# Key norms and low-rank inputs prepared in the value columns, and unread products in four gaps of TensorE

## What is computed

```python
h = rmsnorm(x, lp['norm1_g']) * (1.0 + sc1) + sh1
proj = h @ lp['w_in']
r_a, k_a, v_a, q_b, k_b, v_b, x_c, g_c = jnp.split(proj, SPLIT_POINTS, axis=-1)
...
kk = l2_normalize((k * lp['rwkv_kk']).reshape(shp))
for d in range(2):
    w = jnp.exp(-DECAY_SCALE * jax.nn.sigmoid(lp['rwkv_w0'][d] + jnp.tanh(h @ lp['rwkv_wA'][d]) @ lp['rwkv_wB'][d]))
    a = jax.nn.sigmoid(lp['rwkv_a0'][d] + (h @ lp['rwkv_aA'][d]) @ lp['rwkv_aB'][d])
    kd = k * (1.0 + (a - 1.0) * lp['rwkv_ka'])
    o, s_last = rwkv7_scan(rh, w, kd, vh, kk, a, s0[:, d], reverse=(d == 1))
g = jax.nn.sigmoid(h @ lp['rwkv_gA']) @ lp['rwkv_gB']
```

## Time and profile before

| | us |
|---|---|
| median of 3 runs | 4451.15 |
| the runs | 4451.15, 4453.65, 4433.3 |
| the profiled execution | 4451.32 |
| its span, first to last instruction | 4449.5 |
| mean granted clock of TensorE in it | 0.951 of full rate |
| TensorE busy | 4073.4 (92%) |
| VectorE busy | 3399.8 (76%) |
| ScalarE busy | 1590.9 (36%) |
| GpSimd busy | 1405.3 (32%) |

### The profile page before, as it was taken

The page is one execution under the profiler, slowest core; times in us unless marked ns, Lnnn a source line. Parts: engine busy times, 40 slices in busy tenths (PEclk is TensorE's granted clock), DMA queues, the critical chain, the costliest instruction groups (busy, mean ns, idle before and its releaser), DMA issues. The chain is left out here.

```text
span 4449.5 us, 71520 instructions
## 1 busy us (share of the span) xinstructions
PE 4073.4 (92%) x26630; PEld 3259.4 (73%) x26630; DVE 3399.8 (76%) x6371; ACT 1590.9 (36%) x2620; POOL 1405.3 (32%) x1046
## 2 busy tenths in 40 slices
PE   7988887999998999999979888789999899999997
PEld 5966666766577888888879566577656788888885
DVE  3556544488988999999945566437898899999996
ACT  4424532311165333333343355332113733333333
POOL 0010000054313656666500000002542066566661
PEclk8989878999999999999989799889999999999998
DMA  6230002388989999999921300125997899999994
GB/s 239 70 123 5 2 2 97 132 330 308 327 250 327 409 408 407 404 405 402 356 81 57 122 2 2 60 104 202 320 347 275 254 407 409 408 405 401 404 406 183
DMA packets 412900, 1096.19 MB, mean 246 GB/s; under 512 B 38240, under 2 KB 183904, under 8 KB 405984
## 3 DMA queue, kind: packets, MB, share of 16 engines
q1 hardware_dynamic: 265184, 555.88, 34.8%
q0 software_dynamic: 147456, 536.94, 31.0%
HBM read 1013.25 MB, written 79.43 MB: 246 GB/s over the span
## 5 line engine op out<-in xcount | busy, mean ns | idle before, releaser
L1735 POOL DMA_INDIRECT ring<-peer_u_rows,rows x512 | 657.1, 1283 | 2076.1 <-DVEq L2086 1264.3
L1735 POOL DMA_INDIRECT ring<-peer_v,rows x512 | 723.6, 1413 | 399.4 <-DVE acc L2546 327.0
L1692 PE MATMUL ps<-h,u 128*128 128x384 f32 x2048 | 676.9, 487 | 2.5 <-PEq L1807 2.5
L204 PE MATMUL ps<-vhi,wlo 128*128 128x512 f32 x1536 | 608.7, 396 | 72.7 <-DVE wlo L2525 72.4
L2546 DVE SCALAR_TENSOR_TENSOR acc<-ring,act,acc 128x1024 f32<-128x1024 f32 x508 | 644.7, 1279 | 24.3 <-DMA ring<-peer_v,rows 22.0
L1739 DVE SCALAR_TENSOR_TENSOR ring<-ring,acc 128x1024 f32<-128x1024 f32 x512 | 619.0, 1222 | 25.3 <-DMA ring<-peer_u_rows,rows 24.7
L205 PE MATMUL ps<-vlo,whi 128*128 128x512 f32 x1536 | 604.2, 393 | 0.0
L206 PE MATMUL ps<-vhi,whi 128*128 128x512 f32 x1536 | 603.6, 393 | 0.0
L1692 PEld LDWEIGHTS ps<-h,u 128*128 128x128 f32 x2048 | 382.8, 190 | 252.0 <-issue 2.9
L204 PEld LDWEIGHTS ps<-vhi,wlo 128*128 128x128 f32 x1536 | 292.3, 190 | 147.5 <-issue 88.1
L204 PE MATMUL ps<-xhi,ulo 128*128 128x384 f32 x1024 | 344.9, 337 | 23.1 <-DVE xlo L2503 23.1
(11 more groups left out here) (358 smaller groups left out, 7439.2 us busy)
## 6 DMA issues: line engine op xcount, KB each, us to landing
u<-peer_u SPq DMA_DIRECT2D x256, 512.0 KB, 7.0
v<-peer_v SPq DMA_DIRECT2D x256, 512.0 KB, 6.8
gates<-stage SPq DMA_DIRECT2D x24, 2048.0 KB, 9.6
sel<-gates SPq DMA_DIRECT2D x64, 768.0 KB, 8.3
mod_ring<-mod_late SPq DMA_DIRECT2D x32, 1024.0 KB, 7.6
query_raw<-peer_wq SPq DMA_DIRECT2D x64, 512.0 KB, 3.7
hidden<-hh SPq DMA_DIRECT2D x128, 192.0 KB, 6.9
u<-hidden SPq DMA_DIRECT2D x128, 192.0 KB, 6.0
```

The costliest lines, as they stand in the source:

```text
L204: pe.matmul(out, lhs[1], rhs[0], start=start, stop=False)
L1692: mm = pe.matmul(self.g.ps[:, bank, 0:ND], self.u[:, slot, kc, :], self.x[:, kc, 0:ND], start=(kc == 0), stop=(kc == KC - 1))
L1735: return pool.indirect_dma_start(to, None, table, rows)
```

## The change

Four things change.

1. **Key norms and low-rank inputs.** The sums of squared keys move from `rwkv_prepare` to the value columns of `proj_stage`: ScalarE squares the scaled keys after column 18, TensorE sums them behind the first two value tiles, VectorE limits them, ScalarE makes the inverse root, which stays in the rows X0 and X0 + 1 of `g.proj`. Tanh and Sigmoid of the low-rank inputs move there too, and so does the transfer of `wB`, whose buffer now lives over both stages. In `rwkv_prepare` a single instruction per chunk scales and normalizes the keys.
2. **Decay scale.** The multiplication of all four decay sets by the scale is gone; the exponentials take it as their factor.
3. **One direction on GpSimd.** Of the four sets, sets 2 and 3 (the backward direction) get their key scaling from ScalarE and GpSimd and their bonus product from GpSimd.
4. **Unread products and waits.** `keep_warm` multiplies the identity with a constant of 512 columns into a PSUM bank that nobody reads: 5 times behind the sums of the first norm, 4 times at the end of `mix_stage`, 7 times at the start of `gemm`, 4 times behind the sums of the selection's norm. The wait for the state moves from the start of `mix_stage` to `rhs0`; in `rwkv_prepare` the transfers have semaphores of their own.

```diff
+def keep_warm(g, pe, bank, times):
+    for _ in range(times):
+        pe.matmul(g.ps[:, bank, :], g.ident, g.keep[:, 0:512], start=True, stop=True)
...
@@ gemm, TensorE @@
             before["tensor"](pe)
+            keep_warm(g, pe, 2 * R - 1, 7)
...
@@ proj_stage: SyncE, ScalarE, TensorE @@
+            sync.dma_start(lora[0][:, :, :], d["rwkv_B"][l]).then_inc(lora[1], 16)
...
             for n in range(NPROJ):
                 lru.on_scalar(act, n, taken, vectors)
                 high(n + W)
+                if n == KEYS_AT:
+                    act.wait_ge(lru.conv, CC)
+                    act.wait_ge(taken, PROJ_ORDER.index(K0 + CA - 1) + 1)
+                    for c in range(CA):
+                        nc.scalar.activation(g.proj[:, X0 + c, :], g.proj[:, K0 + c, :], ACT.Square,
+                                             scale=g.v("kk", c, c + 1)).then_inc(key_squared, 1)
+            for c in range(CA):
+                x = g.proj[:, X0 + c, :]
+                act.wait_ge(key_taken, c + 1)
+                nc.scalar.activation(x, x, ACT.Ln).then_inc(key_logs, 1)
+            for c in range(CA):
+                x = g.proj[:, X0 + c, :]
+                act.wait_ge(key_logs, c + 1)
+                nc.scalar.activation(x, x, ACT.Exp, scale=-0.5).then_inc(key_roots, 1)
             for n in range(NPROJ + W, NW):
                 high(n)
+            act.wait_ge(taken, NPROJ)
+            nc.scalar.activation(g.proj[:, LW, :], g.proj[:, LW, :], ACT.Tanh).then_inc(lora_in, 1)
+            nc.scalar.activation(g.proj[:, LG, :], g.proj[:, LG, :], ACT.Sigmoid).then_inc(lora_in, 1)
...
             norm["tensor"](pe)
+            keep_warm(g, pe, 2 * R - 1, 5)
...
+            def key_sums(c):
+                if c:
+                    pe.wait_ge(key_taken, c)
+                else:
+                    pe.wait_ge(lru.gate_tk, 8)
+                pe.wait_ge(key_squared, c + 1)
+                for bank, (x, y) in enumerate(((0, NS), (NS, NT))):
+                    mm = pe.matmul(g.ps[:, 2 * R + bank, 0:y - x], g.bones, g.proj[:, X0 + c, x:y], start=True, stop=True)
+                mm.then_inc(key_summed, 1)
...
-                    if 2 <= n < 2 + ROPE:
-                        rotate(n - 2)
+                    if n < CA:
+                        key_sums(n)
+                    if CA <= n < CA + ROPE:
+                        rotate(n - CA)
...
@@ rwkv_prepare: TensorE, ScalarE, GpSimd, VectorE @@
-            pe.wait_ge(loaded, 48)
+            pe.wait_ge(lora_loaded, 16)
...
-            pe.wait_ge(first, 2)
...
-            for c in range(CA):
-                pe.wait_ge(sq, c + 1)
-                sums(g.bones, squares[c])
+            pe.wait_ge(gb_loaded, 16)
...
+            def key_scale(i):
+                c = i % CA
+                nc.scalar.activation(g.proj[:, KH0 + i, :], aa[:, i, :], ACT.Identity, scale=v("ka", c, c + 1),
+                                     bias=g.omka[:, c:c + 1]).then_inc(scale_in, 1)
...
+            act.wait_ge(z_tk, 8)
+            key_scale(3)
+            key_scale(2)
             exponentials(1)
...
+        @block.gpsimd
+        def _(pool):
+            pool.wait_ge(kk_done, CA)
+            pool.wait_ge(z_tk, 8)
+            for n, i in enumerate((3, 2)):
+                kh = g.proj[:, KH0 + i, :]
+                pool.wait_ge(scale_in, n + 1)
+                pool.tensor_tensor(kh, kh, g.proj[:, K0 + i % CA, :], ALU.mult).then_inc(scaled, 1)
+            for i in (2, 3):
+                pool.wait_ge(logs, 2 * i + 2)
+                pool.tensor_tensor(g.proj[:, BH0 + i, :], kk[:, i % CA, :], aa[:, i, :], ALU.mult).then_inc(bonused, 1)
...
             for c in range(CA):
-                k.then(ve.tensor_scalar(kk[:, c, :], g.proj[:, K0 + c, :], v("kk", c, c + 1), None, ALU.mult))
-                ve.tensor_tensor(squares[c], kk[:, c, :], kk[:, c, :], ALU.mult).then_inc(sq, 1)
+                ve.scalar_tensor_tensor(kk[:, c, :], g.proj[:, K0 + c, :], v("kk", c, c + 1), g.proj[:, X0 + c, :],
+                                        ALU.mult, ALU.mult).then_inc(kk_done, 1)
...
-            ve.wait_ge(z_tk, 4)
-            k.then(ve.tensor_scalar(lw[:, :, :], lw[:, :, :], -DECAY_SCALE, None, ALU.mult))
+            ve.wait_ge(loaded, 16)
             log_sums(0)
...
@@ mix_stage, TensorE @@
-            pe.wait_ge(loaded, 64)
...
+                if (step, name) == (0, "rhs0"):
+                    pe.wait_ge(state_in, 32)
...
+            keep_warm(g, pe, S + 1, 4)
...
@@ select_stage, TensorE @@
             norm["tensor"](pe)
+            keep_warm(g, pe, TURNED, 4)
```

90 lines of the change are left out of this document (38 added, 52 removed).

## The result

The changed kernel takes 4409.03 us (median of 11 runs, 4397.48 to 4438.77) against 4453.65 us before (11 runs, 4433.3 to 4473.11): a ratio of 0.9906 with a 95% interval of 0.9884 to 0.9928, 32 to 52 us less. Forecast were 4408 us. The profiled execution took 4400.1 us, its span 4398.3 us, 51.2 us less than the one of before.

What follows compares the result with a forecast made beforehand. It took a wait for constants and a 12 us transfer pause to set the preparation's end. Terms: -28 (preparation) + 4.4 (value columns) - 7.7 (mixing start) - 2.6 - 3.8 - 3.4 - 2.0 (unread products) = -43.1 us: 4408 us, range 4380 to 4436 us.

Steps and rivals of the forecast that it cites:

- Preparation (-28): rwkv_prepare: earlier low-rank and modulation products end the transfer pause, so the stage ends 14 us earlier per layer.
- the head: Start of the preparation: TensorE no longer waits for constants, first low-rank product 5.6 us earlier in each layer.
- full rate as its consequence: Eight low-rank products in the preparation: at full rate after a short gap, 10 us instead of 14.8 us.
- the norms: Key norms leave TensorE's chain in the preparation, 4.1 us per layer, and appear in the value columns.
- The end of the stream: Preparation's weight transfers: without the 12 us pause they end at 319 us, the stage at 322.5 us in layer 0.
- Whether VectorE is ready: Preparation: VectorE's last group ends near 321 us, under 322.5 us; GpSimd's four products cost 0, bound +4.5 us per layer.
- Value columns (+4.4): Value columns of the projections: two key norms added to TensorE's dense work, +2.2 us per layer, bounds 2.1 and 4.
- Start of the mixing stage (-7.7): Mixing stage's start: TensorE no longer waits for the state, gaining 3.9 and 3.8 us; range 2.9 to 3.9 us.
- Unread products (-11.8): Four idle gaps of TensorE: products hidden, clock mostly holds; terms -2.6, -3.8, -3.4, -2.0 us; bounds 0 and -14 us.
- The mixing stage: Rival: a different share of slow clock there, 0.39 us per microsecond at 1.2 GHz; chance 0.20 for less, 0.10 for more.
- without the long stretch: Rival case: no long stretch of slow clock in the mixing stages, 4381 us; chance 0.20.
- in both layers: Rival case: a long stretch of slow clock in the mixing stages of both layers, 4436 us; chance 0.10.

Runs made afterwards that it cites:

- The head alone: Kernel before, with low-rank weights loaded and Tanh and Sigmoid done a stage earlier, TensorE waiting for these weights alone, key norms left in the preparation: 4449.01 us, ratio 0.998.
- the kernel that has none there: Changed kernel without the unread products behind the mixing stage and ahead of the output projection, those in the two norms kept: 4412.27 us, ratio 0.9911.
- a filled one: Changed kernel with 8 unread products instead of 5 ahead of the projections and 7 instead of 4 behind the mixing stage: 4401.51 us, ratio 0.9877.

## Where the prediction was right and where not

*Preparation (-28): right in its sum, wrong in its split.* It gave 14.5 us in layer 0 (from the barrier at 284.9 us to 322.6 us, 37.7 us, against 52.2 us) and 15.7 us in layer 1. I had put 5.6 us on the head, 4.8 us on full rate as its consequence ("TensorE comes out of dense work with a gap of half a microsecond, so I expect them at full rate"), 4.1 us on the norms. The head alone gave 5.4 and 8.5 us, with that gap and half rate in one of two layers; the norms' move is worth 8.2 to 9.3 us, 3.6 us for the norms themselves, 4.0 us for the full rate that came with it every time, the rest further down the stage. Why it came every time is open. The decay scale (part 2 of the change) was not run by itself. The end of the stream was right: 322.5 us forecast, 322.6 us measured.

*Whether VectorE is ready: right for its end, wrong for GpSimd's part.* The slack of 3 us was there with all the work on VectorE (3.03 us); with GpSimd's half 0.83 us of it is left. GpSimd's products took 1.8 and 2.06 us, inside the bounds (the second over the 2 us that I had named as a sign of being wrong), but none of them was free: 5.4 us of collisions against 4.3 us of work taken over. The Trainium skill, SBUF — State Buffer, section "Who interferes with whom", had this: a VectorE instruction with two inputs in SBUF meets a GpSimd instruction that reads it. By that rule these products gain VectorE nothing, and the trace agrees (0.82 us became 2.16 us). I had weighed it against a median that said nothing of instructions side by side.

*Value columns (+4.4): right.* 2.5 us of TensorE in each layer, with no idle time around them; VectorE's maxima never held them up. At full rate they run from A to their end in 208.8 us; before, 209.5 and 208.2 us with 6 and 3 us of half rate in it.

*Start of the mixing stage (-7.7): right.* TensorE's gain was 4.3 and 4.1 us. VectorE's first product gained 3.1 us (4.5 us behind the preparation's end instead of 7.5 us), at my lower bound, as the second mask came late; but its next group gained 4.1 us, and that is what the stage goes by.

*Unread products (-11.8): wrong in the stretches, and this is the step that failed.* "All are hidden and the clock mostly holds": they were hidden, and it didn't hold. I took from the earlier trace rows that it falls 3.5 us after the last product, with a margin of 0.2 us in the projections' norm. In the changed kernel it fell behind gaps of 3.3 and 2.6 us, and held over one of 2.5 us. Where it falls late, the half-rate stretch lies on the dense products, which are on the path, and not in the gap. By term, forecast for both layers: projections -2.6, measured 0; mix_finish -3.8, measured +1.6 and +2.4 us in this execution (against the kernel that has none there) and about +0.9 us a layer in the mean; output projection -3.4 with up to 1 us late, measured -2.0 us in each layer and not late; the selection -2.0, measured -1.0 us in each layer and right, behind H; besides, its sums, at half rate here as before (11.97 us), are 1.3 us shorter in most other kernels (10.3 to 10.6 us), which I had not forecast. So the failed part is the clock behind the first norm and behind the mixing stage. By the stretches some 5 us of the 11.8 us are there in the mean of the profiled kernels, 3 us up to H and 2 us behind it. The times, 11 and 12 us with standard errors of 5 us, agree with 5 us and with 11.8 us.

*The mixing stage* was a rival and not the forecast, and its sign came: mean clocks of 0.94 and 0.94 instead of 0.86 and 0.96. It is not one of a few cases, as I had it ("without the long stretch", "in both layers"), but a spread from 26 to 105 us of half rate in a stage, in kernels of either kind. The price of 0.39 us was right to within 1.5 us in 28 stages. The profiled execution before had 120 us of it, this one 75 us: 17.5 of its 51.2 us.

*The total*: 34 us outside of the mixing stages against the 43.1 us of the sum. In the stretches up to H the unread products are some 11 us short of their terms (2 us of it come behind H), and the preparation and the start of the mixing stage gave 3 us more than theirs. The 34 us alone would have made a median of 4419 us, which the interval of the ratio, beginning at 32 us, just allows. That it was 4409 us, the forecast, is luck as far as the argument goes: some 10 us come from no term of the sum, be it scatter or the clock of the mixing stages.

## What to carry to other kernels

Where one stage's time is set by a clock that changes from execution to execution, cut the span at instructions that both kernels have, and compare the stretches at equal clock; the total can agree with a sum of which a quarter is wrong. But read a stretch from several executions before a gain of 1 or 2 us is called nothing. Products that nobody reads can just move the half-rate stretch onto work that counts: here a half-filled gap ahead of the projections gained nothing and a filled one 1.3 to 2.8 us, while behind the mixing stage even a filled one gained nothing. Work handed from VectorE to GpSimd was not taken off it here while both read two tensors from SBUF, so hand over what has no VectorE neighbour, or nothing.

## What the runs showed of the hardware

Two things that I had not expected. The granted clock depends on more than the idle time just before it: behind the same gap of 0.79 us and the same nine products it stayed at 2.4 GHz in one layer and fell to 1.2 GHz in the other of one kernel, and at the start of the mixing stage it fell from 1.00 to 0.50 with TensorE busy for 2.1 us of the 3 us before and 3.0 us of the 3 us behind. And a copy of ten elements in a partition with one input, 0.16 us alone, took 1.50 us beside GpSimd's product: what collides isn't only the large instructions with two inputs.
